# A two-layer block in fp32 on one core: gate columns, keys' compression and the turn of the gates issued at other points

## The chip, the cores and the metric

One core of one Trainium2 chip runs the whole program in one launch. The metric is the device time in microseconds of that core; the time of the kernel before is the median of 3 runs.

## The reference

The input is 512 positions of width 2048. Two blocks follow each other; only what the change touches is told in full.

```
mod = silu(c) @ w_ada + b_ada            # shift, scale, gate: 3 x 2048
h = rms_norm(x) * (1 + scale) + shift
xr, gr, qc, kvc, kr, ga = split(h @ w_in)
y_rnn = rg_lru(conv4(xr)) * silu(gr)     # 1024 channels
y_att = mla(qc, kvc, kr) * silu(ga)      # 8 heads
x = x + gate * (concat(y_rnn, y_att) @ w_out)

h = rms_norm(x) * g
q, kv, g_logits, z_a, uv, z_b, merge = split(h @ w_in_2)
kc, vc = compress(k_c), compress(v_c)    # silu(blocks of 32 @ w1) @ w2
gates = sigmoid(g_logits)                # 3 x 16 heads
o_a = (gates0 * attend(q, kc, vc) + gates1 * attend(q, ks, vs)
       + gates2 * attend(q, kw, vw)) * silu(z_a)
o_b = spatial_gating(uv) * silu(z_b)
x = x + (g_a * (o_a @ up_a) + g_b * (o_b @ up_b)) @ w_out_2
x = x + sigmoid(x @ w_ple_gate) * (p @ w_ple)
out = rms_norm(x) * final_g
```

`gate` is the third part of `mod`: 2048 numbers that multiply the output of the first block. `compress` runs once over keys and once over values.

## The kernel before

**The stream of weights.** All large weights come from DRAM as 365 and some more blocks of 128x1024 floats, in one fixed order, the list PLAN. SyncE issues their transfers into slots (`raw`). Each block that TensorE multiplies in full precision is split: ScalarE copies it rounded into the upper half `whi` (L1146), GpSimd takes the difference as the lower half `wlo` (L2496). TensorE then makes three products for each 128x128 piece, upper by upper, upper by lower and lower by upper: L535, L536, L538 with the weights held, or L531, L532, L534 with the activations held (`token_blocks`). There are three pairs of halves; `split_plan` works out in advance at which block each split is issued (`SPLIT_AT`), and `use()` on ScalarE and GpSimd issues them.

**The order of the work.** Each engine has its own function (`tensor`, `scalar`, `vector`, `gpsimd`, `sync`), whose instructions run in the order in which they are written; semaphores join them. Beside the main run over the blocks, each engine keeps a list of generators (`jobs`). A `tick()` takes one step of each, and `project` has one `tick()` between the two halves of a block row. An attention unit is such a job: scores, an empty step, transposes, an empty step, then the values together with the next head's scores. In this way small matmuls and softmaxes are laid in between the large products. PSUM banks are handed out in turn: ring "main" has two, ring "side" five; a claim waits for whoever emptied the bank last.

**Three places.** (1) *Gate columns.* During the first block's projections, blocks of `w_ada` for `gate` are multiplied by VectorE into `gac` (L1737, L1740), eight blocks for each of four groups g = 8 to 11. After the last one TensorE sums over partitions with four narrow matmuls (L879, `ada_sum`), and VectorE adds the bias (L1747, `ada_bias`). The groups end at c = 3 and c = 7 of the first loop and at h = 2 and h = 6 of the second. (2) *Compression.* TensorE multiplies KC by the compression's weights (L970), first for keys (kv = 0), then for values (kv = 1). The job `compressed(kv)` then does the rest: VectorE reads the offset (L2198, L2199), ScalarE makes a tanh into HID (L1512), VectorE turns it into silu (L2203, L2205), TensorE multiplies by W2 (L945 for keys, L951 for values) and VectorE copies out (L2213, L2218). The keys' L945 stands on TensorE behind the values' L970. Behind it come the weights `w2sv` (L531 to L534). (3) *Turn of the gates.* After the 48 wide block `w2g`, ScalarE takes the tanh into GF (L1552), TensorE transposes it (L999), ScalarE copies it to GT (L1555), VectorE scales it (L2258). Then the job `attention2` begins: L1015 and L1030 are its scores, BT (L1569) its tables on ScalarE, L2288, L1577 and L2304 its softmax, L1042 its transposes; SC is the compressed scores' tile, cleared once by L2330 and first written at L2340.

Of the kernel before, what the change touches and what calls it, by code (L numbers as in the profile page):

```python
# [9 lines left out]
ACT = mybir.ActivationFunctionType  # L10
AX = mybir.AxisListType

P = 128
# [278 lines left out]
def build(nc, wst, xt, crow, pos, vec, cst, lrw, w2bd, selb, sgw, rows, pt, x1s, tgs, pls, out):  # L292
    ctx = ExitStack()
    with ctx:
# [28 lines left out]
        def C(name):  # L323
            a, b = CST[name]
            return ct[:, a:b]
# [97 lines left out]
        GT = at(M0 + 91.25, 192, F, "GT")  # L423
        GF = area(95, 1, "GF")
# [33 lines left out]
        def up(sem, *key, frees=None, by=1):  # L458


            T.up(sem, key, frees, by)
            return S[sem], by

        def done(*key):

            return T.place[key] if T.known else T.place.get(key, ("vec", 0))
# [5 lines left out]
        def claim(b, *key):  # L472


            before = T.holder.get(b)
            T.holder[b] = key
            T.bank_of[key] = b
            return banks[b], T.freed.get(before, []) if T.known and before is not None else []

        def bank(*key):  # L480
            return banks[T.bank_of.get(key, 0)]
# [23 lines left out]
        def tensor(e):  # L505
            w = Waits(e, S)
            turn = {"main": 0, "side": 0, "use": 0}
            jobs = []

            def tick():  # L510
                for g in list(jobs):
                    if next(g, jobs) is jobs:
                        jobs.remove(g)

            def ring(name):
                turn[name] += 1
                of = (0, 1) if name == "main" else (2, 3, 4, 5, 6)
                return of[(turn[name] - 1) % len(of)]
# [363 lines left out]
            def gates():  # L882
                for g in range(8, 12):
                    for j in range(8):
                        chunk("ada", g, j)
                        if j < 7:
                            yield
                    o, prior = claim(ring("side"), "gate", g)
                    ada_sum(g, o, prior)
                    yield  # L890

            gate_it = gates()
            for c in range(8):
                project("win1", c, "h")
                for _ in range(GATED[2 * c]):
                    next(gate_it)
                jobs.insert(0, recurrence(c))
                tick()
                project("win1", 8 + c, "h")
                for _ in range(GATED[2 * c + 1]):  # L900
                    next(gate_it)
                tick()
            for h in range(8):
                project("win1", 25 + h, "h")
                for _ in range(GATED_LATE[h]):
                    next(gate_it)
                tick()
                if h == 2:
                    while jobs:
                        tick()  # L910
# [80 lines left out]
                m = three(o[0:48, :], hi[:, ws], lo[:, ws], HT[kt][0], HT[kt][1], kt == 0, kt == 15, c)  # L991
            m.then_inc(*up("used_pe", "used", c))
            T.place["proj", "w2g", 0] = T.place["used", c]
            o, prior = claim(ring("side"), "gt")
            w.wait_ge(*done("gf"))
            for f in prior:
                w.wait_ge(*f)
            for b in range(4):
                m = e.transpose(o[:, 48 * b:48 * b + 48], GF[0:48, b * P:(b + 1) * P], C("ident")[0:48, 0:48])  # L999
            m.then_inc(*up("tr_pe", "gt"))  # L1000
            while jobs:
                tick()


            def attention2():
                for t_i, (a_, r_) in enumerate(PAIRS2):
# [81 lines left out]
                    yield  # L1088
                    values(1)

            jobs.append(attention2())

            for g in range(8):
# [36 lines left out]
        def scalar(e):  # L1130
# [4 lines left out]
            def tick():  # L1135
                for g in list(jobs):
                    if next(g, jobs) is jobs:
                        jobs.remove(g)
# [9 lines left out]
            def use(n=1):  # L1148
                for _ in range(n):
                    halves(SPLIT_AT[turn["use"]])  # L1150
                    turn["use"] += 1
# [361 lines left out]
                    *up("cmp_act", "cmpt", kv, frees=("cmp", kv)))  # L1513
                yield

            for kv in range(2):
                use(4)
                jobs.append(compressed(kv))
                tick()
            for half in range(2):  # L1520
                use(8)
                after1()
# [18 lines left out]
            for i in range(12):  # L1541
# [9 lines left out]
            w.wait_ge(*done("proj", "w2g", 0))  # L1551
            e.activation(GF[0:48, :], bank("proj", "w2g", 0)[0:48, :], ACT.Tanh, scale=0.5).then_inc(  # L1552
                *up("tanh_act", "gf", frees=("proj", "w2g", 0)))
            w.wait_ge(*done("gt"))
            e.activation(GT[:, :], bank("gt")[:, 0:192], ACT.Copy).then_inc(*up("evac_act", "gtc", frees=("gt",)))  # L1555
            while jobs:
                tick()

# [62 lines left out]
            jobs.append(attention2())  # L1621
            for g in range(8):
                use()
                tick()
                use()
                w.wait_ge(*done("proj", "w2f", 16 + g))
                e.activation(sub(OB, g), bank("proj", "w2f", 16 + g)[:, :], ACT.Gelu_apprx_tanh).then_inc(
                    *up("gelu_act", "u", g, frees=("proj", "w2f", 16 + g)))
                tick()
                use()  # L1630
                tick()
                use()
                w.wait_ge(*done("proj", "w2f", 24 + g))
                w.wait_ge(*done("uv", g))
                e.activation(SU[0][:, :], bank("proj", "w2f", 24 + g)[:, :], ACT.Tanh, scale=0.5).then_inc(
                    *up("tanh_act", "zb", g))
                tick()
# [56 lines left out]
        def vector(e):  # L1694
# [409 lines left out]
            gate_it = gates()  # L2104
            for c in range(8):
                tick()
                jobs.insert(0, recurrence(c))
                tick()
                tick()
                for _ in range(GATED[2 * c] + GATED[2 * c + 1]):  # L2110
                    next(gate_it)
                w.wait_ge(*done("gr", c))
                e.scalar_tensor_tensor(g3[:, :], g3[:, :], 1.0, bank("proj", "win1", 8 + c)[:, :], ALU.add,
                                       ALU.mult).then_inc(*up("gate_dve", "sg", c, frees=("proj", "win1", 8 + c)))
                gate_columns()
                sg["c"] = c - 1
                tick()
                sg["c"] = c
            for h in range(8):
                y = sub(QN, h)  # L2120
                g = za[h % 2][:, :]
                for _ in range(GATED_LATE[h]):
                    next(gate_it)
                tick()
                if h == 7:
                    for k in range(8):
                        lower(k, sub(YR, k), "y", [done("y", k), done("used", INDEX["win1", 32, 0])])
                w.wait_ge(*done("ga", h))
                e.scalar_tensor_tensor(g, g, 1.0, bank("proj", "win1", 25 + h)[:, :], ALU.add, ALU.mult).then_inc(
                    *up("gate_dve", frees=("proj", "win1", 25 + h)))  # L2130
                w.wait_ge(*now("gate_dve"))
                w.wait_ge(*done("o1", h))
                e.scalar_tensor_tensor(y, g, 0.5, y, ALU.mult, ALU.mult).then_inc(*up("gate_dve", "y", 8 + h))
                gate_columns()
                tick()
                if h == 2:
                    while jobs:
                        tick()
# [807 lines left out]
```

## Time and profile before

| what | value |
|---|---|
| median of 3 runs | 2467.18 us (2466.94 to 2468.97) |
| profiled execution, its own time | 2467.53 us |
| its span, first to last instruction | 2465.8 us |
| TensorE busy | 2406.8 us (98%) |
| GpSimd, VectorE, ScalarE busy | 984.5, 930.2, 822.7 us |
| mean granted clock of TensorE | 0.991 |
| DMA | 309.55 MB, 126 GB/s |

Busy time of TensorE is taken from the start of an instruction to its modelled end, so pieces overlap: in a stream of 512 column matmuls each row says 0.39 us, while one starts every 0.23 us. A wait stands in brackets in the timeline, with the instruction that ended it. The granted clock is a share of 2.4 GHz: 1.00 is 2.4, 0.50 is 1.2.

### The profile page before, as it was taken

What the parts mean: (1) busy time and instruction counts of PE and PEld (TensorE: products, weight loads), DVE (VectorE), ACT (ScalarE), POOL (GpSimd) and SP (SyncE); (2) the same over time, 40 slices, a digit from 0 to 9 for tenths busy, and PEclk for the clock granted to TensorE, in tenths of its full rate; (3) what the DMA queues carried; (4) which work ended last, traced back from release to release, by engine and by line L of the source; (5) the groups of instructions that cost most, each with busy time, mean ns of one, the idle gap of its engine ahead of it and who ended that gap; (6) DMA issues with size and microseconds to landing.
All of it is one profiled execution on the core that took longest, in us unless ns stands there. A gap on an engine that the chain in (4) does not pass through costs nothing.

```text
span 2465.8 us, 28169 instructions
## 1 busy us (share of the span) xinstructions
PE 2406.8 (98%) x11092; PEld 1906.4 (77%) x11092; DVE 930.2 (38%) x1485; ACT 822.7 (33%) x1267; POOL 984.5 (40%) x426
## 2 busy tenths in 40 slices
PE   7899999999999999999999999999999999999996
PEld 4567677778888888887887778787878888888885
DVE  4764466566500620210555534343421412202113
ACT  5245444442322332222434333333322312213321
POOL 1344333234555434443332324242434444444553
PEclk9899999999999999999999999999999999999998
DMA  8962233236444343232222323232333444454332
GB/s 294 402 245 79 60 133 108 90 107 210 150 150 135 116 161 95 88 101 87 67 86 60 93 83 107 86 109 84 108 95 102 154 146 128 131 167 121 93 103 85
DMA packets 98435, 309.55 MB, mean 126 GB/s; under 512 B 10624, under 2 KB 12032, under 8 KB 98176
## 3 DMA queue, kind: packets, MB, share of 16 engines
q1 hardware_dynamic: 98304, 307.76, 38.8%
q8 instruction: 88, 1.44, 0.3%
q14 instruction: 43, 0.35, 0.0%
HBM read 285.69 MB, written 20.97 MB: 124 GB/s over the span
## 4 chain that ended last, share of the span: by engine, by line
PE 89%; DVE 5%; ACT 2%; issue 2%; DMA 1%; SPq 1%; POOL 0%; DVEq 0%; ACTq 0%; POOLq 0%
PE bank L535 24%; PE bank L538 24%; PE bank L536 24%; PE bank L531 2%; PE bank L532 2%; PE bank L534 2%; PE bank L1030 2%; PE bank L1054 1%; PE bank L1042 1%; DVE hlo L1708 1%; DMA raw<-in_wst 1%; PE bank L829 1%; PE bank L840 1%; DVE hlo L2428 1%; DMA rawx<-in_wst 1%
## 5 line engine op out<-in xcount | busy, mean ns | idle before, releaser
L2496 POOL TENSOR_TENSOR wlo<-raw,whi 128x1024 fp32r<-128x1024 f32 x365 | 895.1, 2457 | 1248.2 <-ACT whi L1146 1240.2
L535 PE MATMUL bank<-hhi,whi 128*128 128x512 f32 x2752 | 1087.6, 395 | 19.9 <-ACT whi L1146 17.2
L538 PE MATMUL bank<-hhi,wlo 128*128 128x512 f32 x2752 | 1078.0, 392 | 7.3 <-POOL wlo L2496 7.3
L536 PE MATMUL bank<-hlo,whi 128*128 128x512 f32 x2752 | 1075.4, 391 | 0.0
L535 PEld LDWEIGHTS bank<-hhi,whi 128*128 128x128 f32 x2752 | 518.2, 188 | 144.5 <-ACT whi L1146 18.9
L538 PEld LDWEIGHTS bank<-hhi,wlo 128*128 128x128 f32 x2752 | 517.9, 188 | 123.0 <-POOL wlo L2496 13.1
L536 PEld LDWEIGHTS bank<-hlo,whi 128*128 128x128 f32 x2752 | 518.5, 188 | 106.6 <-issue 0.7
L1146 ACT ACTIVATE whi<-raw 128x1024 fp32r<-128x1024 f32 x365 | 384.5, 1055 | 594.8 <-PE bank L538 482.4
L2304 DVE TENSOR_SCALAR S<-S,sm 128x512 f32<-128x512 f32 (+1 forms) x64 | 78.0, 1218 | 0.6
L531 PE MATMUL bank<-whi,hhi 128*128 128x512 f32 x192 | 76.0, 396 | 0.0
L532 PE MATMUL bank<-whi,hlo 128*128 128x512 f32 x192 | 75.7, 394 | 0.0
L534 PE MATMUL bank<-wlo,hhi 128*128 128x512 f32 x192 | 75.6, 394 | 0.0
L1577 ACT ACTIVATE S<-S,sm 128x512 f32<-128x512 f32 (+1 forms) x64 | 35.3, 551 | 119.1 <-DVE sm L2294 119.1
L2304 DVE TENSOR_SCALAR S2b<-S2b,sm 128x512 f32<-128x512 f32 (+1 forms) x64 | 73.6, 1150 | 0.0
L2469 DVE SCALAR_TENSOR_TENSOR tgt<-tgt,MG 128x512 f32<-128x512 f32 x16 | 11.1, 693 | 141.6 <-ACT tgt L1683 141.6
L2288 DVE CUSTOM_DVE_ANT_0 S<-bank,BT 128x512 f32<-128x512 f32 (+1 forms) x64 | 31.2, 487 | 87.3 <-PE bank L1030 87.2
L2156 DVE SCALAR_TENSOR_TENSOR X<-bank,sm,axr 128x512 f32<-128x512 f32 x16 | 12.0, 750 | 137.6 <-PE bank L538 137.6
L2461 DVE TENSOR_TENSOR X<-bank,axr 128x512 f32<-128x512 f32 x16 | 11.0, 690 | 138.4 <-PE bank L538 138.4
L2320 DVE COPY PT<-bank 128x384 f32<-128x384 f32 (+2 forms) x48 | 20.0, 417 | 96.6 <-PE bank L1042 96.6
L2496 POOL TENSOR_TENSOR wlo<-rawx,whi 128x1024 fp32r<-128x1024 f32 x11 | 31.0, 2835 | 54.1 <-ACT whi L1146 41.5
L1646 ACT ACTIVATE TS<-bank 128x512 f32<-128x512 f32 x32 | 18.9, 591 | 99.9 <-PE bank L538 94.5
L1763 DVE CUSTOM_DVE_ANT_0 junk<-rawx,cB,sm 128x1024 f32<-128x1024 f32 x19 | 42.1, 2218 | 5.3 <-DMA rawx<-in_wst 4.7
(308 smaller groups left out, 2110.5 us busy)
## 6 DMA issues: line engine op xcount, KB each, us to landing
raw<-in_wst SPq DMA_DIRECT2D x397, 512.0 KB, 3.6
rawx<-in_wst SPq DMA_DIRECT2D x54, 512.0 KB, 6.8
rawy<-in_wst SPq DMA_DIRECT2D x26, 512.0 KB, 4.5
tgs<-TS SPq DMA_DIRECT2D x32, 256.0 KB, 4.0
axr<-tgs SPq DMA_DIRECT2D x32, 256.0 KB, 3.9
X<-in_xt SPq DMA_DIRECT2D x4, 1024.0 KB, 15.3
pls<-stg SPq DMA_DIRECT2D x16, 256.0 KB, 9.5
axr<-in_xt SPq DMA_DIRECT2D x16, 256.0 KB, 2.9
```

The costliest lines, as they stand in the source:

```text
L531: e.matmul(o, xh, hi, start=first, stop=False)
L532: e.matmul(o, xl, hi, start=False, stop=False)
L534: return e.matmul(o, xh, lo, start=False, stop=last)
L535: e.matmul(o, hi, xh, start=first, stop=False)
L536: e.matmul(o, hi, xl, start=False, stop=False)
L538: return e.matmul(o, lo, xh, start=False, stop=last)
L1030: e.matmul(bks[n][0][:, off:off + wd], qq[pb:pb + 64, P * i:P * (i + 1)], kk[pb:pb + 64, 0:wd], start=True, stop=True).then_inc(*up("score ...
L1146: e.activation(sub(whi, PAIR[c], CH), slots[slot(c)], ACT.Copy).then_inc(*up("whi_act", "whi", c))
L1577: e.activation(sl, sl, ACT.Exp, scale=SM2, bias=smx[:, 8 + k:9 + k], accum_out=smx[:, 16 + k:17 + k]).then_inc(*up("exp_act", "exp", u, gb ...
L1763: e.tensor_tensor_reduce(out=junk[:, :], in0=slots[slot(c)], in1=cB[:, 1024 * i:1024 * (i + 1)], scale=0.5, scalar=half[:, 0:1] if i else ...
L2304: e.tensor_scalar(sl, sl, ri[:, 4 * gb + i:4 * gb + i + 1], None, ALU.mult, ALU.bypass).then_inc(*up("soft_dve", "soft", u, gb, i))
L2496: e.tensor_tensor(sub(wlo, PAIR[c], CH), slots[slot(c)], sub(whi, PAIR[c], CH).bitcast(F), ALU.subtract).then_inc(*up("wlo_pool", "wlo", c))
```

## The change

On TensorE the sum of a gate group is taken out of the generator `gates` and put into `gate_columns`, which is called after the `tick()` that follows. VectorE's bias for it is moved too: in the first loop behind the next `tick()`, in the second to the start of the next step. On ScalarE `compressed(0)` is called before the `use()` of the eight compression blocks and not between the first four and the last four. On TensorE the turn of the gates becomes a job, ahead of `attention2`, so it runs at the tick in the middle of the next block row; ScalarE's copy of it moves behind the `use()` of that row.

```diff
@@ tensor
                 for g in range(8, 12):
                     for j in range(8):
                         chunk("ada", g, j)
-                        if j < 7:
-                            yield
+                        if j == 7:
+                            summed.append(g)
+                        yield
+            def gate_columns():
+                while summed:
+                    g = summed.pop()
                     o, prior = claim(ring("side"), "gate", g)
                     ada_sum(g, o, prior)
-                    yield
...
                 for _ in range(GATED[2 * c + 1]):
                     next(gate_it)
                 tick()
+                gate_columns()
...
                 for _ in range(GATED_LATE[h]):
                     next(gate_it)
                 tick()
+                gate_columns()
...
-            o, prior = claim(ring("side"), "gt")
-            w.wait_ge(*done("gf"))
-            ...
-            m.then_inc(*up("tr_pe", "gt"))
             while jobs:
                 tick()
+            def gate_turn():
+                o, prior = claim(ring("side"), "gt")
+                w.wait_ge(*done("gf"))
+                ...
+                m.then_inc(*up("tr_pe", "gt"))
+                yield
...
+            jobs.append(gate_turn())
             jobs.append(attention2())
@@ scalar
-            for kv in range(2):
-                use(4)
-                jobs.append(compressed(kv))
-                tick()
+            jobs.append(compressed(0))
+            tick()
+            use(8)
+            jobs.append(compressed(1))
+            tick()
...
-            w.wait_ge(*done("gt"))
-            e.activation(GT[:, :], bank("gt")[:, 0:192], ACT.Copy).then_inc(*up("evac_act", "gtc", frees=("gt",)))
...
             for g in range(8):
                 use()
+                if g == 0:
+                    w.wait_ge(*done("gt"))
+                    e.activation(GT[:, :], bank("gt")[:, 0:192], ACT.Copy).then_inc(
+                        *up("evac_act", "gtc", frees=("gt",)))
                 tick()
@@ vector
             for c in range(8):
                 tick()
+                gate_columns()
                 jobs.insert(0, recurrence(c))
...
-                gate_columns()
                 sg["c"] = c - 1
...
             for h in range(8):
...
+                gate_columns()
                 for _ in range(GATED_LATE[h]):
                     next(gate_it)
...
-                gate_columns()
                 tick()
```

How the order of instructions moves is shown at three places (the changed program's line numbers are a little higher: L1740 becomes L1757, L1747 becomes L1764, L1146 becomes L1160, L1512 becomes L1526).

VectorE at the first gate group (c = 3), before: `gac` is the accumulation, L1747 the bias, S the next softmax.

```order
L1740 SCALAR_TENSOR_TENSOR gac<-rawy_105,sm,gac 128x512 x2
L2113 SCALAR_TENSOR_TENSOR g_156<-g_156,bank 128x512
L1747 TENSOR_TENSOR sm<-bank,vt 128x4
L2077 SCALAR_TENSOR_TENSOR g_154<-YR,g_154 128x512
L2080 SCALAR_TENSOR_TENSOR YR<-g_153,g_154 128x512
L2085 SCALAR_TENSOR_TENSOR YR<-g_156,YR 128x512
```

And with the change:

```order
L1757 SCALAR_TENSOR_TENSOR gac<-rawy_105,sm,gac 128x512 x2
L2131 SCALAR_TENSOR_TENSOR g_156<-g_156,bank 128x512
L2094 SCALAR_TENSOR_TENSOR g_154<-YR,g_154 128x512
L2097 SCALAR_TENSOR_TENSOR YR<-g_153,g_154 128x512
L2102 SCALAR_TENSOR_TENSOR YR<-g_156,YR 128x512
...
L2035 TENSOR_SCALAR S_150<-bank,sm 128x256
L1764 TENSOR_TENSOR sm<-bank,vt 128x4
L2076 TENSOR_SCALAR xc<-bank,vt 128x512
```

The bias moved behind the next softmax; the accumulation stayed where it was. On TensorE these six rows stand around the sum in both programs, with the same numbers in the order:

```order
L536 MATMUL bank<-hlo,whi 128x512
L538 MATMUL bank<-hhi,wlo 128x512
L879 MATMUL bank<-ct,gac 128x1 x4
L535 MATMUL bank<-hhi,whi 128x512
L536 MATMUL bank<-hlo,whi 128x512
L538 MATMUL bank<-hhi,wlo 128x512
```

Nothing moved there, at this group nor at the other three.

ScalarE at the compression, before:

```order
L1157 ACTIVATE hhi<-unb_189 128x512
L1146 ACTIVATE whi<-raw 128x1024 x2
L1512 ACT_TABLE_LOAD
L1512 ACTIVATE HID<-bank,sm 128x62
L1146 ACTIVATE whi<-raw 128x1024
L1512 ACTIVATE HID<-bank,sm 128x62
L1146 ACTIVATE whi<-raw 128x1024 x7
```

And with the change:

```order
L1171 ACTIVATE hhi<-unb_189 128x512
L1526 ACT_TABLE_LOAD
L1526 ACTIVATE HID<-bank,sm 128x62
L1160 ACTIVATE whi<-raw 128x1024 x3
L1526 ACTIVATE HID<-bank,sm 128x62
L1160 ACTIVATE whi<-raw 128x1024 x7
```

The keys' tanh, with its table load, went ahead of two upper halves; the values' tanh kept its place behind the third.

TensorE at the turn of the gates, with the change (before, L999 stood ahead of the 24 matmuls of the half block whose last two are shown first, right behind the 48 wide block):

```order
L536 MATMUL bank<-hlo,whi 128x512
L538 MATMUL bank<-hhi,wlo 128x512
L1013 MATMUL bank<-ct,GF 128x48 x4
L1028 MATMUL bank<-KCT,Q_190 128x64 x4
L1043 MATMUL bank<-KS,Q_190 128x512 x2
```

The turn now stands right in front of attention's first scores.

## Rows read from the trace of the kernel before

**Rows 1.** The page's totals: busy us, share of the span, instructions.
```profile
PE 2406.8 (98%) x11092; PEld 1906.4 (77%) x11092; DVE 930.2 (38%) x1485; ACT 822.7 (33%) x1267; POOL 984.5 (40%) x426
```

**Rows 2.** TensorE's waits by line: us in total, times, longest.
```profile
PE bank L879 <- DVE gac L1740: 5.3, 2, 2.6
PE bank L945 <- DVE HID L2205: 4.0, 1, 4.0
```

**Rows 3.** Busy time by stretch: us, five engines' busy, granted clock, DMA share, GB/s.
```profile
429.30:432.80 3.50, 3.50 (x10) 2.72 (x9) 3.36 (x3) 0.00 (x0) 1.17 (x1) 0.51 0.94 364
556.60:560.00 3.40, 3.39 (x19) 2.99 (x20) 2.82 (x5) 0.04 (x1) 0.00 (x0) 1.00 0.74 233
886.80:893.60 6.80, 5.66 (x14) 4.56 (x15) 2.23 (x8) 0.95 (x2) 4.42 (x3) 0.50 1.01 404
```

**Rows 4.** Timeline at the first gate group: start, duration, engine, instruction, [wait].
```profile
422.45 4.52 DVE L1740 SCALAR_TENSOR_TENSOR gac<-rawy,sm,gac 128x512 f32<-128x512 f32 x4
...
427.03 1.05 PE L879 MATMUL bank<-ct,gac 128*128 128x1 f32 x8 [2.64 <-DVE gac L1740]
```

**Rows 5.** Timeline of the compression, all engines, 876.5 to 900 us.
```profile
876.30 7.65 PE L970 MATMUL bank<-KC,rawz 128*128 128x93 f32 x67
...
876.91 0.15 DVE L2199 TENSOR_SCALAR sm<-bank 128x1 f32<-128x1 f32 x1
...
882.03 1.06 ACT L1146 ACTIVATE whi<-raw 128x1024 fp32r<-128x1024 f32 x1 [7.97 <-DMA raw<-in_wst]
883.16 6.96 POOL L2496 TENSOR_TENSOR wlo<-raw,whi 128x1024 fp32r<-128x1024 f32 x3 [26.00 <-ACT whi L1146]
...
884.89 1.28 ACT L1512 ACT_TABLE_LOAD   x1
886.18 0.31 ACT L1512 ACTIVATE HID<-bank,sm 128x62 f32<-128x62 f32 x1
...
887.94 0.69 PE L945 MATMUL bank<-HID,W 128*128 128x62 f32 x2 [4.00 <-DVE HID L2205]
...
888.39 0.78 PE L531 MATMUL bank<-whi,hhi 128*128 128x512 f32 x1
...
889.39 0.63 PE L534 MATMUL bank<-wlo,hhi 128*128 128x512 f32 x1
...
893.63 0.40 PE L531 MATMUL bank<-whi,hhi 128*128 128x512 f32 x1
...
899.98 0.39 PE L532 MATMUL bank<-whi,hlo 128*128 128x512 f32 x1
```

**Rows 6.** Timeline of the turn of the gates, 1164 to 1173 us.
```profile
1164.42 0.39 PE L538 MATMUL bank<-hhi,wlo 128*48 128x512 f32 x1
1165.49 0.45 PE L999 MATMUL bank<-ct,GF 48*128 48x48 f32 x4 [0.68 <-ACT GF L1552]
1165.87 0.50 PE L535 MATMUL bank<-hhi,whi 128*128 128x512 f32 x1
...
1166.60 0.27 DVE L2330 MEMSET SC<- 128x256 f32 x1
...
1171.44 1.00 PE L1015 MATMUL bank<-KCT,Q 128*128 128x64 f32 x8
1172.48 0.48 DVE L2340 SCALAR_TENSOR_TENSOR SC<-ct,bank 128x124 f32<-128x124 f32 x2 [5.61 <-PE bank L1015]
```

**Rows 7.** Timeline of attention's first softmax beside GpSimd.
```profile
1182.88 2.70 POOL L2496 TENSOR_TENSOR wlo<-raw,whi 128x1024 fp32r<-128x1024 f32 x1 [13.16 <-ACT whi L1146]
1183.23 2.50 DVE L2304 TENSOR_SCALAR S<-S,sm 128x256 f32<-128x256 f32 x1
1185.66 0.41 DVE L2304 TENSOR_SCALAR S2b<-S2b,sm 128x384 f32<-128x384 f32 x1
...
1191.07 0.28 DVE L2304 TENSOR_SCALAR S2b<-S2b,sm 128x128 f32<-128x128 f32 x1
...
1197.63 0.27 PE L1042 MATMUL bank<-ct,S 128*128 128x128 f32 x1
```

More of the change, by code:

```diff
@@ L885, in gates @@
                         chunk("ada", g, j)
-                        if j < 7:
-                            yield
+                        if j == 7:
[4 more added lines that the diff above has]
+                    g = summed.pop()
                     o, prior = claim(ring("side"), "gate", g)
                     ada_sum(g, o, prior)
-                    yield
+            summed = []
             gate_it = gates()
@@ L993, in tensor @@
             T.place["proj", "w2g", 0] = T.place["used", c]
-            o, prior = claim(ring("side"), "gt")
-            w.wait_ge(*done("gf"))
[L996 to L999, printed above, removed]
-            m.then_inc(*up("tr_pe", "gt"))
             while jobs:
                 tick()
+            def gate_turn():
+                o, prior = claim(ring("side"), "gt")
+                w.wait_ge(*done("gf"))
+                for f in prior:
+                    w.wait_ge(*f)
+                for b in range(4):
+                    m = e.transpose(o[:, 48 * b:48 * b + 48], GF[0:48, b * P:(b + 1) * P], C("ident")[0:48, 0:48])
+                m.then_inc(*up("tr_pe", "gt"))
+                yield
             def attention2():
```

## The prediction

> **What bounds the kernel now.** I read the page's totals first: TensorE is busy for 2406.8 of 2465.8 us [rows 1], so about 59 us are left to win in all, and only time in which TensorE stands still or runs slowly counts. The view of TensorE's waits comes next. Of its rows, two belong to what the diff touches: 5.3 us in two waits at L879, which adds up the gate columns, and 4.0 us in one wait at L945, the second product of the keys' compression [rows 2]. The turn of the gates at L999 has 0.68 us [rows 6]. The other waits stand at places that the diff leaves alone. Last I read the granted clock beside these places: 0.50 for 6.8 us after the wait at L945, 0.51 for 3.5 us after one wait at L879, but 1.00 after the other, which was as long (the two make 5.3 us, the longest 2.6) [rows 2, 3]; between 556.6 and 560.0 TensorE runs behind that other one. 0.5 is 1.2 GHz of 2.4. So a wait costs its own length and sometimes a slow stretch behind it.
>
> **Gate columns.** The words of the change say that they are added up behind the attention's next steps. The order of TensorE's instructions says otherwise: the ticks past which the sum is moved issue nothing there, since attention's four-tick pattern has an empty step at each of the four places. L879 stands between the same matmuls as before, all four times. VectorE's accumulation, four products in 4.52 us, starts at 422.45 and ends at 426.97 (422.45 + 4.52), and TensorE goes on at 427.03 [rows 4]. None of these instructions moves. What moves is VectorE's addition of the bias, one instruction of 128x4 at two of the four places (behind the next softmax, and behind the scan). VectorE no longer stands before it until the sum is there; its next user of the bank on TensorE also needs the convolution, which VectorE issues after the bias, so no new wait forms. I take 0 us. The bounds are 0 and -5.3 us, the two waits of [rows 2] gone.
>
> **Compression.** The chain that TensorE waits for at L945 is: keys' products end, VectorE copies the offset (until 877.06), ScalarE loads a table (1.28 us) and computes the tanh (0.31), VectorE multiplies twice, L945 starts at 887.94 [rows 5]. Between 877 and 884.89 ScalarE has only two upper halves to do, at 882.03 and right after, and the first waits for a transfer to land. The tanh stands behind both, so it is late because of a DMA with which it has nothing to do. The change puts the tanh ahead of them. It can start at about 877.1, is done at 878.7, and VectorE, which has nothing else to do there, has finished before 880. The halves lose nothing, as their data comes at 882.03. TensorE reaches L945 at 883.95, where the values' products end (the row that starts at 876.30 lasts 7.65) [rows 5], and does not wait.
> What is late next? After L945 (0.45 us until L531) TensorE begins the next weights at 884.40. Its third matmul, L534, needs the lower half. GpSimd makes three from 883.16 in 6.96 us, so the first is there at 883.16 + 6.96 / 3 = 885.48 [rows 5]. L534 then starts at about 885.55, where 884.86 would be possible: some 0.7 us of a new wait take the place of the old one. Before, that L534 started at 889.39. Gain 889.39 - 885.55 = **3.84 us**. The second and third lower halves (887.8 and 890.1) are needed only 5.4 us apart from 890.6 on.
> The slow stretch: from the L534 at 889.39 to the L531 at 893.63 stand 10 steps in 4.24 us [rows 5]; at full clock, from 893.63 to 899.98, 28 steps take 6.35 us, 0.227 each [rows 5], so 10 take 2.27. If the clock stays up, this gives another **1.97 us**. I take it, because the stand before it shrinks from 4.00 to 0.7 us, and even 2.6 us with short matmuls behind it left the clock at 1.00 in one case of two [rows 2, 3]. Bounds: 0 and -1.97.
> How long the first lower half takes is the one open size. VectorE, which stood still in that stretch, now has four small operations in it. At 1182.88 a lower half took 2.70 us beside VectorE's work [rows 7], so 0.36 us more is the other bound; I keep 2.34, since it starts at 883.16 and VectorE's first of them follows L945, after 884. The Trainium skill (SBUF — State Buffer, "SBUF: two separate sides") says that VectorE and GpSimd share one pair of ports as an exclusive lock, and that whoever starts first holds it for the whole instruction. By that rule too it would be 2.34 us and not 2.70.
>
> **Turn of the gates.** Before, the last L538 of the gates' block starts at 1164.42, TensorE waits for the tanh, turns (L999), and the next block's L535 starts at 1165.87: 1.45 us [rows 6]. Now that L535 follows after one step of 0.227, and L999 comes 24 matmuls later, where its input has long been there; it costs 1165.87 - 1165.49 = 0.38 us. Gain 1.45 - 0.23 - 0.38 = **0.84 us**. Behind it the copy of the gates, VectorE's scaling and the clearing of SC come half a block later. Counted from L999 the clearing ends at 1166.87 - 1165.49 = 1.38 us. In the new order L1015 follows L999 by 0.38, and VectorE's first use comes 1172.48 - 1171.44 = 1.04 us after L1015, that is 1.42 us after L999 [rows 6]: it just fits. ScalarE's upper half that was queued behind the copy is now ahead of it. Price 0; the other bound is that the softmax's chain starts later by all of the 1.38 us, which the slack of 6.3 us in front of its transposes (below, rival d) covers.
>
> **Sum.** 0 + 3.84 + 1.97 + 0.84 = 6.65 us. TensorE is the bound for all that follows, so this is kept to the end. The profiled execution took 2467.53 us around its span of 2465.8, and gives 2460.9; the median shown (2467.18) lies 0.35 lower, so I say 2460.5.
>
> **Rivals.**
> (a) The clock falls at the compression anyway. For it: both slow stretches of [rows 3] follow a stand with short matmuls beside it, and L945 with L970 in front of it (93 columns) stay. Against it: the stand is 0.7 us. It gives back 1.97: 2462.5. The Trainium skill (TensorE: Matmul & The Clock Gate, "A second HAM failure mode: psum-queue depth-cycling") says that frequent small stands between groups of matmuls can be enough to make the clock swing. By that rule this rival would be the likely one; no row here shows a fall after a stand as short as 0.7 us.
> (b) The compression gains little, because the transfer or the first lower half comes later: the upper half at 882.03 stood waiting for a DMA [rows 5]. Every microsecond later is one less, at 2 us 2462.5 with the clock up.
> (c) The two gate waits go as the words promise. 5.3 us of waits and a slow stretch of 3.5 us, worth 1.6 us, would give 2453.6. Against it stands the unchanged order on TensorE; something on VectorE would have to be 2.6 us earlier.
> (d) Slower: attention's softmaxes fall badly against GpSimd. VectorE's scaling L2304 takes 0.41 us where GpSimd rests and 2.50 where it works [rows 7]. In the first unit its last one ends at 1191.35, and TensorE's transposes start at 1197.63: 6.3 us of slack, which three more blocked operations at 2.50 - 0.41 = 2.09 us use up. From the fourth on TensorE waits. Six of the 16 units with four more would cost 6 x 2.09 = 12.5, net +5.9: 2473.1. Against it: all engines are paced by TensorE, and the new offsets within the first unit are under 0.1 us.
> (e) The compression stays as it is, because the tanh at L1512 needs something that comes late too: 2466.3, the turn alone. Its inputs in the trace are there at 877.06.
>
> **Chances.** Forecast as summed 0.70; (a) 0.11; (b) 0.08; (c) 0.04; (d) 0.03; (e) 0.04. The measurement of this kernel tells about 0.2%, 4.9 us, from no change, so "faster" starts below 2462.25. The forecast and (c) lie there, and a part of (a) and (b), where the slow stretch that follows L879 in this execution is absent in others: faster 0.77, same 0.20, slower 0.03. The range takes in (a), most of (b) and the 0.36 us above, and below a slow stretch of the gate columns that fails to come (1.6 us): 2458.6 to 2463.3. The runs shown differ by 2.0 us among themselves, which is about such a stretch.
>
> **What would show it.** In the profile after: L945 without a wait, and one of 0.5 to 1 us for the lower half at the L534 behind it; ScalarE's tanh at about 877 to 879; granted clock 1.00 from 884 to 894; L999 without a wait, half a block later, at about 1164.3 in the new times; the two waits of 2.64 us at L879 unchanged; no new wait in attention. Wrong would be: L879's waits gone or longer, a wait at L1042 or at L538 near 1180, or a clock of 0.5 behind the compression.

## The result and the profile after

| | median | range | runs |
|---|---|---|---|
| before, same rounds | 2468.97 us | 2465.6 to 2470.1 | 13 |
| changed | 2462.59 us | 2461.47 to 2465.56 | 13 |

The ratio is 0.9979, with a 95% interval of 0.9972 to 0.9986: 5.2 us less, between 3.5 and 6.9. The medians differ by 6.4. The profiled execution of the changed kernel took 2465.56 us, the slowest of its 13, with a span of 2463.8: only 2.0 us under the profile of before. Where the rest of the gain is in that one execution is the main thing to see below. All ratios are of fast runs; a single run of the kernel before in later rounds took 7219.94 us, at a granted clock of 1.00 and unexplained, and is left out of them (the median of its set is 2468.24 with it and 2468.18 without).

TensorE's waits by line, changed kernel (us in total, times, longest; L879 is the gate columns, L534 the first use of a lower half behind the compression):

```profile
PE bank L535 <- ACT whi L1160: 16.5, 4, 9.9
PE bank L538 <- POOL wlo L2513: 7.2, 6, 1.7
PE bank L879 <- DVE gac L1757: 5.3, 2, 2.6
...
PE bank L534 <- POOL wlo L2513: 1.1, 1, 1.1
```

Against [rows 2], L945's 4.0 us are gone, 1.1 us have come at L534, and L879 has its 5.3 us as before. The turn of the gates is no longer in the list.

Timeline of the compression, changed kernel (L1526 is the keys' tanh, L1160 an upper half, L2513 the lower halves, L954 what was L945):

```profile
880.68 1.28 ACT L1526 ACT_TABLE_LOAD   x1 [2.83 <-PE bank L979]
...
881.97 0.31 ACT L1526 ACTIVATE HID<-bank,sm 128x62 f32<-128x62 f32 x1
...
882.71 0.23 DVE L2222 SCALAR_TENSOR_TENSOR HID<-HID 128x62 f32<-128x62 f32 x1
...
886.03 1.06 ACT L1160 ACTIVATE whi<-raw 128x1024 fp32r<-128x1024 f32 x1 [3.74 <-DMA raw<-in_wst]
887.16 7.06 POOL L2513 TENSOR_TENSOR wlo<-raw,whi 128x1024 fp32r<-128x1024 f32 x3 [26.23 <-ACT whi L1160]
...
887.58 0.36 PE L954 MATMUL bank<-HID,W 128*128 128x62 f32 x2
887.75 0.48 PE L531 MATMUL bank<-whi,hhi 128*128 128x512 f32 x1
...
889.58 0.50 PE L534 MATMUL bank<-wlo,hhi 128*128 128x512 f32 x1 [1.12 <-POOL wlo L2513]
```

The tanh is done at 882.28 and silu at 882.94, 4.6 us before TensorE wants it; in [rows 5] it came last. The bound there is now the transfer of the first block, which lets ScalarE begin at 886.03, and the lower half that follows from it.

Timeline of the turn, changed kernel:

```profile
1168.55 0.44 PE L1013 MATMUL bank<-ct,GF 48*128 48x48 f32 x4
1168.92 1.10 PE L1028 MATMUL bank<-KCT,Q 128*128 128x64 f32 x8
1169.03 0.33 ACT L1639 ACTIVATE GT<-bank 128x192 f32<-128x192 f32 x1 [4.30 <-PE bank L1013]
...
1169.65 0.27 DVE L2347 MEMSET SC<- 128x256 f32 x1
...
1170.07 0.48 DVE L2357 SCALAR_TENSOR_TENSOR SC<-ct,bank 128x124 f32<-128x124 f32 x2
```

No wait on TensorE at L1013, and VectorE's first use of SC comes 0.15 us after the clearing, 1.15 us after L1028 (1.04 before, [rows 6]).

Busy time by stretch, changed kernel (the columns of [rows 3]; the clock stands third from the end):

```profile
430.00:434.80 4.80, 4.80 (x13) 3.74 (x12) 2.81 (x2) 0.00 (x0) 1.04 (x1) 0.50 0.99 369
561.20:564.60 3.40, 3.40 (x10) 2.63 (x9) 3.11 (x6) 0.98 (x1) 0.00 (x0) 0.50 0.95 363
884.00:889.50 5.50, 4.46 (x38) 4.03 (x37) 0.66 (x4) 2.54 (x3) 2.34 (x2) 1.00 1.01 374
889.50:896.00 6.50, 6.42 (x28) 5.33 (x29) 1.48 (x2) 1.42 (x3) 5.78 (x4) 1.00 1.02 408
```

The compression runs at full clock, where [rows 3] had 0.50 for 6.8 us. But behind the two waits at L879, which are the same as before to the hundredth, this execution ran at half clock for 6.8 us (428.0 to 434.8) and for 3.4, where the one of before did for 3.4 and not at all.

Starts at fixed points show what that cost. First to second sum at L879: 558.78 - 427.62 = 131.16 us, before 129.58. Second to third: 37.48, before 35.83. Together 3.2 us lost where the code of TensorE is the same, and 0.6 more before the first sum, 0.5 of it in the first 45 us. From the end of the values' products to the tenth step behind the first L534: 893.63 - 883.95 = 9.68 us before, and 889.58 + 2.27 - 887.58 = 4.27 now, 5.4 less. From the last L538 of the gates' block to attention's first product: 7.02 us before, 1168.92 - 1162.77 = 6.15 now, 0.9 less. So the two stretches that the change acts on are shorter by 6.3 us, and this execution gave 3.8 of it back elsewhere, 3.2 of it by the clock. Whether the change has a part in that is not shown by one profile; the runs speak against a loss of 3.2 us in every execution, which would leave 3.1 us, outside the 3.5 to 6.9 measured.

### The profile page after: what moved, and what is told of

Its sections match the earlier page's. It is cut to its first block, busy times and chain, and to the rows that moved or that the text cites. A ratio compares the mean times of both kernels' runs of the same rounds, so it can differ in the third digit from the quotient of the medians.

```text
span 2463.8 us, 28169 instructions
## 1 busy us (share of the span) xinstructions
PE 2409.3 (98%) x11092; PEld 1907.1 (77%) x11092; DVE 925.2 (38%) x1485; ACT 822.7 (33%) x1267; POOL 985.9 (40%) x426
## 4 chain that ended last, share of the span: by engine, by line
PE 89%; DVE 5%; ACT 2%; issue 2%; DMA 1%; SPq 1%; POOL 0%; DVEq 0%; POOLq 0%; ACTq 0%
PE bank L535 24%; PE bank L538 24%; PE bank L536 24%; PE bank L531 2%; PE bank L534 2%; PE bank L532 2%; PE bank L1043 2%; PE bank L1067 1%; PE bank L1055 1%; DVE hlo L1725 1%; DMA raw<-in_wst 1%; PE bank L829 1%; PE bank L840 1%; DVE hlo L2445 1%; DMA rawx<-in_wst 1%
## 5 line engine op out<-in xcount | busy, mean ns | idle before, releaser
L2513 POOL TENSOR_TENSOR wlo<-raw,whi 128x1024 fp32r<-128x1024 f32 x365 | 896.5, 2461 | 1246.6 <-ACT whi L1160 1238.3
L538 PE MATMUL bank<-hhi,wlo 128*128 128x512 f32 x2752 | 1078.7, 392 | 7.3 <-POOL wlo L2513 7.2
L538 PEld LDWEIGHTS bank<-hhi,wlo 128*128 128x128 f32 x2752 | 518.9, 189 | 123.6 <-POOL wlo L2513 13.1
L1160 ACT ACTIVATE whi<-raw 128x1024 fp32r<-128x1024 f32 x365 | 384.5, 1055 | 588.7 <-PE bank L538 482.7
L534 PE MATMUL bank<-wlo,hhi 128*128 128x512 f32 x192 | 74.8, 390 | 1.1 <-POOL wlo L2513 1.1
L2513 POOL TENSOR_TENSOR wlo<-rawx,whi 128x1024 fp32r<-128x1024 f32 x11 | 30.9, 2826 | 53.3 <-ACT whi L1160 41.7
```

Source lines behind the costliest of these rows:

```text
L534: return e.matmul(o, xh, lo, start=False, stop=last)
L538: return e.matmul(o, lo, xh, start=False, stop=last)
L1160: e.activation(sub(whi, PAIR[c], CH), slots[slot(c)], ACT.Copy).then_inc(*up("whi_act", "whi", c))
L2513: e.tensor_tensor(sub(wlo, PAIR[c], CH), slots[slot(c)], sub(whi, PAIR[c], CH).bitcast(F), ALU.subtract).then_inc(*up("wlo_pool", "wlo", c))
```

## The experiments

Theory: the compression gives nearly all, the turn 0.8, the gate columns nothing, since their sum stays where it was on TensorE. Rivals: the gates carry part of the gain; the slow stretches have nothing to do with the waits. The first three kernels are one part of the change each.

**Compression alone** (`compress_only`), against the kernel before:

```diff
-            for kv in range(2):
-                use(4)
-                jobs.append(compressed(kv))
-                tick()
+            jobs.append(compressed(0))
+            tick()
+            use(8)
+            jobs.append(compressed(1))
+            tick()
```

> Only the keys' tanh goes ahead of the first upper halves; gate columns and the turn are as before. My theory: this part carries the gain, 3.8 us of wait and 2.0 us of slow clock less, so 5.8 us under the kernel before in the same rounds, and L945 without a wait. Rival (the three parts share the gain, or the gates carry it): 2 us or less.

Measured: 2462.9 us (2461.1 to 2466.32, 11 runs) beside 2467.73 for before (27 runs); ratio 0.998 (0.9972 to 0.9989), 4.9 us less, between 2.7 and 6.9. In the profile L945 doesn't wait, and L534 waits 1.5 us. The theory's 5.8 lies inside; the rival's 2 does not.

**Turn alone** (`turn_only`): the parts of the change's diff that hold `gate_turn` and the copy to GT.

> Only the turn of the gates goes half a block later. My theory: 0.8 us less, within what the runs can tell from nothing; the wait of 0.68 us at the turn is gone in the profile and none comes in its place. Rival (attention's first softmax starts late and TensorE waits for it): 0 or above, with a wait at L1042 or at L538 near 1180 us.

Measured: 2467.95 us (11 runs), ratio 1.0001 (0.9993 to 1.001). That includes 0.8 us less and nothing. The profile decides; the timeline of TensorE, turn alone:

```profile
1164.93 0.39 PE L538 MATMUL bank<-hhi,wlo 128*48 128x512 f32 x1
...
1170.71 0.44 PE L1004 MATMUL bank<-ct,GF 48*128 48x48 f32 x4
1171.09 0.43 PE L1019 MATMUL bank<-KCT,Q 128*128 128x64 f32 x2
```

From the block's last L538 to attention's first product 6.16 us, before 7.02: 0.86 less, without a wait between 1160 and 1200 us. At the scores' next line (L1030 before, L1034 here) 0.76 is left of it, since the first two of attention's products now start 0.16 us apart and not 0.06. The step is as large as said to within 0.1 us, and too small for run times to show.

**Gate columns alone** (`gates_only`): the parts that hold `summed` and `gate_columns`.

> Only the gate columns are moved as in the change. My theory: nothing, the two waits of 2.64 us at L879 stay, and the time is that of the kernel before within 1 us. Rival (the bias that no longer stands before VectorE's scan brings something): 0.6 us or more. Rival (the bias behind the softmax makes a new wait): slower, with a wait at L870.

Measured: 2468.16 us (11 runs), ratio 1.0004 (0.9995 to 1.0013). L879 waits 5.3 us in two waits of 2.6 as before. The interval is -1.2 to +3.2 us and can't show a zero; the profile does: from the first sum to the second TensorE needs 129.55 us (129.58 before), from the second to the third 35.87 (35.83).

What would take these waits away? On VectorE the accumulation stands behind a step of the recurrence and the copies of attention, and ahead of that step VectorE stood still for 4.5 us. VectorE's timeline, kernel before:

```profile
418.57 0.69 DVE L2067 SCALAR_TENSOR_TENSOR g<-g,xc 128x512 f32<-128x512 f32 x1 [4.53 <-ACT g L1406]
```

**Accumulation earlier** (`accumulate_earlier`), on the changed kernel:

```diff
                 jobs.insert(0, recurrence(c))
                 tick()
-                tick()
                 for _ in range(GATED[2 * c] + GATED[2 * c + 1]):
                     next(gate_it)
+                tick()
```

> The change as it is, and VectorE's accumulation of the gate columns ahead of the recurrence's second step in the first loop, where VectorE stood waiting for ScalarE for 4.5 us. My theory: the waits at L879 come from the accumulation being issued too late on VectorE, so both go (5.3 us) and with them the slow stretches of 3.4 to 6.8 us behind them (1.6 to 3.2 us each where they come): 5.3 to 11 us under the change, some 2455. Rival (the accumulation delays the recurrence, and TensorE waits for its next step or for the last y): the same as the change or slower, with a wait at L870, L810 or at L535 on y.

Measured: 2451.67 us (2450.83 to 2453.24, 5 runs), ratio to before 0.9935 (0.9923 to 0.9948), and 10.9 us under the changed kernel's median. That one was measured in other rounds; against the kernel before of its own rounds each, this one is 16.0 us less and the change 5.2, which is 10.8 apart. L879 has gone from the list of waits, and no slow stretch is left between 72 and 2430 us. VectorE's timeline in this kernel, at the first group:

```profile
410.77 3.55 DVE L1757 SCALAR_TENSOR_TENSOR gac<-rawy,sm,gac 128x512 f32<-128x512 f32 x4
415.39 0.69 DVE L2084 SCALAR_TENSOR_TENSOR g<-g,xc 128x512 f32<-128x512 f32 x1 [1.07 <-ACT g L1420]
```

TensorE's timeline:

```profile
421.05 0.95 PE L879 MATMUL bank<-ct,gac 128*128 128x1 f32 x8
```

The four products end at 414.3, TensorE's sum follows at 421.05 without a wait, and the recurrence still waits for ScalarE, so it lost nothing. The products also take 3.55 us in place of 4.52 [rows 4]: there one of GpSimd's lower halves ran until 424.00, 1.55 us into them, here one ran until 411.35, 0.58 us into them.

The two profiles are 14.7 us apart at TensorE's last product, more than the medians. Of this, 10.7 lie between 400 us and the fourth sum: the two waits of 2.64 and the two stretches at half clock, worth 4.8, make up 10.1 of it. Another 3.1 lie between 45 and 110 us, where the two programs are the same.

**The same on the kernel before** (`before_accumulate`): the diff above, without the change.

> The kernel before, and only VectorE's accumulation ahead of the recurrence's second step; none of the three parts of the change. My theory: the place of the sum on TensorE is of no account, and the accumulation's place alone takes both waits and slow stretches away: the same 10 to 11 us that it brought on top of the change, so about 2457, and L945 still waits 4.0 us. Rival (the bias moved by the change is needed for it, since VectorE would stand before it): 2 us less of it, with a wait of VectorE at L1747.

Measured: 2457.16 us (2455.5 to 2460.69, 4 runs) beside 2468.24; ratio 0.9956 (0.9943 to 0.997), 10.9 us less, between 7.4 and 14.1. VectorE doesn't wait at L1747. So the accumulation's place brings the gain without any part of the change, and with the kernel of the gates alone, where the sum's and the bias's places brought nothing, it is all that mattered here. L945 waits 4.7 us, as its code is that of before; behind that wait the clock was at half for 3.4 us, where it was for 6.8 behind 4.0 [rows 3].

**Are the slow stretches the waits' doing?** (`fill_stand`) On the changed kernel, products that nobody reads fill most of each wait:

```diff
                     o, prior = claim(ring("side"), "gate", g)
+                    if g < 10:
+                        for f in prior:
+                            w.wait_ge(*f)
+                        for _ in range(10):
+                            e.matmul(o[:, :], HT[0][0][:, 0:P], HT[0][0], start=True, stop=True)
                     ada_sum(g, o, prior)
```

> The change, and on TensorE ten products of 512 columns (into the bank that the sum then overwrites) ahead of the sum at the first two gate groups, 2.3 us of work in each wait of 2.64 us. Nothing of the result comes from them. My theory: the waits cost their 5.3 us as before, but the slow stretches behind them (3.4 to 10.2 us together in the profiles so far, worth 1.6 to 4.8 us) follow from TensorE's standing still, so the clock stays at 1.00 after both, and the time is 2 to 4 us under the change. Rival (the clock falls for another reason at these places, the transfers that run there or the narrow matmuls): the slow stretches stay and the time is that of the change.

Measured: 2456.72 us (2455.71 to 2460.05, 5 runs), 5.9 us under the changed kernel's median, though the first sum starts no earlier. All five runs lie under the fastest of the changed kernel's 13; against the kernel before of its own rounds it is 10.9 us less (0.9956), and the change 5.2. TensorE's timeline at the first group, waits filled:

```profile
424.83 2.43 PE L899 MATMUL bank<-hhi 128*128 128x512 f32 x10
427.63 1.05 PE L879 MATMUL bank<-ct,gac 128*128 128x1 f32 x8 [0.38 <-DVE gac L1762]
```

By stretch, first the changed kernel behind its first wait, then this one behind both:

```profile
427.50:434.80 7.30, 7.18 (x22) 5.93 (x23) 5.28 (x5) 1.09 (x2) 2.37 (x1) 0.54 0.92 326
```

```profile
427.50:434.80 7.30, 7.17 (x34) 5.88 (x35) 5.33 (x5) 1.11 (x2) 2.40 (x1) 1.00 0.88 307
555.40:562.00 6.60, 6.42 (x32) 5.47 (x33) 6.24 (x11) 1.27 (x2) 0.00 (x0) 1.00 0.83 290
```

The sum starts at 427.63 as in the changed kernel (427.62), and the clock is 1.00 behind it, where it was 0.54, in spite of much the same transfers (DMA share 0.88 and 0.92) and the same narrow products. So at these two places it falls because TensorE stood still. The second sum comes at 555.58, 3.2 us earlier, and the third at 591.45, 1.6 us further ahead: a slow stretch of 6.8 us costs 3.2 us, one of 3.4 us 1.6. More than the 2 to 4 us expected came in the medians; the profiles, one of each kernel, show 4.8 of it.

**A stand of middle length** (`tanh_between`), on the changed kernel, ScalarE:

```diff
-            jobs.append(compressed(0))
-            tick()
-            use(8)
+            use(3)
+            two = SPLIT_AT[turn["use"]]
+            halves(two[:1])
+            jobs.append(compressed(0))
+            tick()
+            halves(two[1:])
+            turn["use"] += 1
+            use(4)
```

> The change, but with the keys' tanh between the two upper halves, so that it follows the first one, which waits for its transfer. My theory (TensorE's wait at L945 is as long as the tanh is late): the table load starts at the end of that half, some 1.8 us earlier than before the change, so L945 waits about 1.7 us in place of 0 (the change) and 4.0 (before); the lower half is then there in time, so the price against the change is about 1 us if the clock stays at 1.00 behind it, and up to 3 us with a slow stretch. Rival (L2222 is kept off by GpSimd's lower half): the wait is 3 us or more.

Measured: 2463.83 us (10 runs), ratio to before 0.9981 (0.9972 to 0.999); 1.2 us above the changed kernel's median, which the runs can't tell from nothing; so what follows rests on one profile. The chain and the clock, tanh between the halves:

```profile
884.58 0.31 ACT L1526 ACTIVATE HID<-bank,sm 128x62 f32<-128x62 f32 x1
...
885.83 0.43 PE L954 MATMUL bank<-HID,W 128*128 128x62 f32 x2 [2.23 <-DVE HID L2227]
```

```profile
887.40:890.80 3.40, 3.40 (x10) 2.63 (x9) 0.87 (x2) 0.00 (x0) 3.40 (x3) 0.50 1.00 393
```

The wait is 2.2 us (1.7 expected, 0 and 4.0 at the ends), so the tanh's place sets it; the rival's 3 us or more did not come. A stretch of 3.4 us at half clock followed it. In the six profiles in which the tanh comes first (changed kernel, compression alone, accumulation earlier, waits filled and the two below), no such stretch stands there, though L534 waits 0.8 to 1.7 us in five of them.

**Who makes the first block late?** (`rows_later`) On top of the earlier accumulation, SyncE:

```diff
+            load(INDEX["w2sv", 3, 0])
+            e.dma_start(SW[:, :], sgw).then_inc(*up("sgw", by=16))
+            load(INDEX["w2sv", 7, 0])
             e.dma_start(LNG[:, :], rows[0:1, :].to_broadcast([P, 1024])).then_inc(*up("rows", by=16))
             ...
-            e.dma_start(SW[:, :], sgw).then_inc(*up("sgw", by=16))
```

> As accumulate_earlier, and on SyncE the transfers of SW, LNG, LNB and BS (512 KB each) behind one and five more blocks of weights. My theory: they share the DMA engines with the first blocks of w2sv and make them late; without them the first upper half comes about 2 us earlier and the wait of 1.0 us at the L534 behind L945 goes: 1 us under accumulate_earlier. Rival (the first block is late because of the compression's blocks ahead of it): the wait stays and the time is the same.

Measured: 2452.88 us (2450.66 to 2456.16, 5 runs), not faster. My theory fell: the wait at L534 is 1.7 us, longer than the 1.0 it was to take away. Timeline, these transfers later:

```profile
868.51 2.32 SPq L2614 DMA_DIRECT2D raw<-in_wst  x4
...
876.49 1.06 ACT L1160 ACTIVATE whi<-raw 128x1024 fp32r<-128x1024 f32 x1 [4.96 <-DMA raw<-in_wst]
...
880.04 0.50 PE L534 MATMUL bank<-wlo,hhi 128*128 128x512 f32 x1 [1.71 <-POOL wlo L2513]
```

Issued at 868.51, the first block is there at 876.49, 8.0 us later. With the other transfers in their old place (`accumulate_earlier`) it took 6.6 us:

```profile
860.80 3.90 SPq L2614 DMA_DIRECT2D rawz<-in_wst  x3
864.81 1.32 SPq L2614 DMA_DIRECT2D raw<-in_wst  x3
...
871.44 1.06 ACT L1160 ACTIVATE whi<-raw 128x1024 fp32r<-128x1024 f32 x1 [3.62 <-DMA raw<-in_wst]
```

So these transfers were not what made it late; why it took 1.4 us longer without them is not shown. The rows above its issue show what stood ahead of it, the compression's last three blocks (`rawz`). In that kernel SyncE waited three times for L979, which frees their slots (us in total, times, longest):

```profile
SPq L2614 <- PE bank L979: 30.0, 3, 27.2
```

**The first blocks ahead** (`weights_ahead`), again on top of the earlier accumulation, SyncE:

```diff
+            first = INDEX["cmp", 1, 1]
+            of = list(range(len(PLAN)))
+            of[first:first + 6] = [*range(first + 3, first + 6), *range(first, first + 3)]
...
-                    c = turn["ld"]
+                    c = of[turn["ld"]]
```

> As accumulate_earlier, and on SyncE the transfers of the first three blocks of w2sv ahead of the last three of the compression, which wait for their slots in the meantime. My theory: the first upper half is late because its transfer stands in SyncE's queue behind these three and is then in flight with them; moved ahead it lands before 874, ScalarE splits it right behind the keys' tanh, and the wait of 1.0 us at the L534 behind L945 goes. 1 us under accumulate_earlier, which only the profile can show. Rival (the transfers crowd out the compression's own blocks): a wait at L979.

Measured: 2449.99 us (2448.95 to 2452.8, 5 runs), ratio to before 0.9927 (0.9914 to 0.9941): the fastest kernel of the study, 12.6 us under the changed one, which ran in other rounds. Its timeline:

```profile
868.27 0.31 ACT L1526 ACTIVATE HID<-bank,sm 128x62 f32<-128x62 f32 x1
868.48 2.94 ACT L1160 ACTIVATE whi<-raw 128x1024 fp32r<-128x1024 f32 x3
...
869.61 7.04 POOL L2513 TENSOR_TENSOR wlo<-raw,whi 128x1024 fp32r<-128x1024 f32 x3 [22.40 <-ACT whi L1160]
...
874.05 0.48 PE L531 MATMUL bank<-whi,hhi 128*128 128x512 f32 x1
```

The halves follow the tanh at once, L534 is no longer among the waits, and the rival's wait at L979 did not come. So the block was late because it stood in SyncE's queue behind three that waited for their slots. The 1.7 us between the two medians lie within the runs' spread; only the profile shows this step, 1.3 us less from the last of the values' products to the same product some 15 us on.

## Why the prediction was right or wrong

**What bounds the kernel** was right in kind, and incomplete in one respect: I read the clock behind each wait from one execution and took it as given. I also read it only beside the three places, and not in the first 100 us (see the sum).

**Gate columns: 0 us.** Right. Read from the order, not from the words of the change; alone they are at 1.0004, with the waits unchanged. Rival (c) is out.

**Compression: 3.84 + 1.97.** Right in mechanism. The wait at L945 and the slow stretch are gone, and the wait for the lower half came where it was foretold, 1.1 us (1.5 in the kernel with this part alone) where I had 0.7: the first block landed later against TensorE's arrival, 1.55 us ahead of L954 and not 1.92. That makes 5.4 us in place of 5.8. Of its two bounds the lock did not matter (the three lower halves took 7.06 / 3 = 2.35 us each on average), rivals (a) and (e) did not happen, and (b) did by these 0.4 us. The 1.97 is itself one execution's: in the four profiles with a wait of 4.0 to 4.7 us here, the clock was at half for 6.8 us in three and for 3.4 in one. The rule of the Trainium skill (TensorE: Matmul & The Clock Gate, "A second HAM failure mode: psum-queue depth-cycling") on which (a) leaned is not borne out at this place by six profiles with waits of 0 to 1.7 us; at 2.2 us the clock did fall. But elsewhere it did after a wait of no more than 1.7 us (with one of 0.6 us some 2.4 us ahead of it), and the trace of before showed it. TensorE's wait near 88 us and the clock behind it, kernel before:

```profile
88.13 0.79 PE L538 MATMUL bank<-hhi,wlo 128*128 128x512 f32 x1 [1.69 <-POOL wlo L2496]
```

```profile
88.10:91.40 3.30, 3.27 (x13) 1.74 (x14) 3.27 (x4) 1.06 (x1) 1.66 (x1) 0.50 1.03 412
```

The same in compression alone:

```profile
86.28 0.50 PE L538 MATMUL bank<-hhi,wlo 128*128 128x512 f32 x1 [1.70 <-POOL wlo L2497]
```

```profile
86.30:89.60 3.30, 3.30 (x19) 2.27 (x20) 3.17 (x5) 1.06 (x1) 0.89 (x1) 1.00 1.03 415
```

Of the eleven profiles, all with this wait, seven have 3.4 or 6.8 us at half clock here and four have none. So six profiles at the compression don't show that a wait of 1.1 to 1.7 us is always harmless there.

**Turn: 0.84.** Right, 0.86 and 0.87 in two profiles up to attention's first product, 0.76 behind it. The slack that "just fits" did: 0.15 us were left. Rival (d) did not happen; no wait came in attention.

**The sum** of the local parts is 6.3 us against 6.65, and the measured change 5.2 (3.5 to 6.9). The step that failed is the last one, from the sum to a level: "the median shown (2467.18) lies 0.35 lower, so I say 2460.5". In four larger sets the median of the kernel before was 2468.97, 2467.73, 2468.24 and 2468.51; three runs had come out low, by 0.6 to 1.8 us. From 2468.97 the same sum gives 2462.3, and 2462.59 was measured. The profile of before was a low one at the gate columns too: one slow stretch of 3.4 us behind two waits. The others with these waits had 3.4 (gates alone, turn alone) or 6.8 and 3.4 (changed kernel, compression alone, tanh between), worth 1.6 or 4.8 us. The largest difference stands where nothing changes in any of these kernels: for the same products between 45 and 110 us of the trace of before, TensorE took 61.6 to 66.2 us in the eleven profiles (65.0 in the one of before), with 10.2 to 23.9 us in all at half clock in the first 100. That is 4.6 us between executions, where the runs of one kernel differ by 4 to 7. I had allowed for the gate columns' stretch to fail below, but neither for it to grow above nor for those of the first 100 us, which I put at nothing without a reason, so the range's upper end, 2463.3, was too low: 5 of the 13 runs lie over it, and the profiled execution does by 2.3 us. Its centre came from three runs and its width from one execution's stretch; the median of 13 lies inside it, 2.1 us above the forecast. It also lies 0.3 us above 2462.25, below which the prediction calls a time faster (0.77), though the ratio's interval, all of it under 1, does tell it from no change.

## What to carry to other kernels

A name for a change is no evidence of what it does: the sum "behind attention's next steps" stood where it had stood, and the wait went only when its producer moved, into time in which its engine was idle (10.9 us). Cost a wait of the engine that bounds the kernel with its clock: 5.3 us of waits held back some 11 us here, and the part behind them varies from one execution to the next, so a gain of a few us is read from distances between fixed points of two profiles, and a level is only forecast from more than three runs. When a wait is for data, look at what stands in front of the transfer in its queue before blaming what runs beside it.

## What the hardware showed that I had not expected

- In six profiles the first of the two waits of 2.64 us was followed by 3.4 or 6.8 us at half clock (1.2 GHz) and the second by 0 or 3.4, with the same products on TensorE up to there. Of these six, the three with the longer falls are the three that move the keys' tanh, 450 us further on in the program; one profile of each can't tell that from chance. Such a stretch costs a little under half its length (3.2 and 1.6 us). 2.3 us of products nobody reads, put into each wait, kept the clock at 1.00 in the one profile taken, and the kernel was 5.9 us faster. Near 88 us a wait of 1.7 us was followed by 0, 3.4 or 6.8 us at half clock.
- Four equal products of VectorE took 4.52 us where a lower half on GpSimd ran on for 1.55 us, and 3.55 us where it did for 0.58; in both the first product ended 0.55 us after the lower half, and the others took 0.75 us each. The Trainium skill (SBUF — State Buffer, "SBUF: two separate sides") says that VectorE with two inputs in SBUF and GpSimd block each other for a whole instruction; the trace of before agrees: of the eight products between 391 and 427 us the median took 0.75 us and the longest 2.09.
- A block of 512 KB took 8.0 us from its issue to its use with three more, SW's and the compression's last blocks issued around it, and 6.6 us with 1.5 MB of other transfers issued right behind it as well: taking these out of the way did not make it come sooner.
